# A hybrid attention backbone on one core: order of transposes, score products and output projection slices in layer 1's attention

## What is computed

```python
def attend_gqa(q, k, v):
    s = jnp.einsum('bqhgd,bkhd->bhgqk', q, k).astype(jnp.float32) * HEAD_SCALE
    p = jax.nn.softmax(s, axis=-1).astype(v.dtype)
    return jnp.einsum('bhgqk,bkhd->bqhgd', p, v)

# neighbourhood_attention, per row block:
        s_loc = jnp.einsum('bjqhd,bijkhd->bhjqik', q_row, k_sub).astype(jnp.float32) * HEAD_SCALE
        s_loc = jnp.where(col_mask[:, :, None, :], s_loc + bias[None].astype(jnp.float32), NEG_INF)
        s_ctx = jnp.einsum('bjqhd,bkhd->bhjqk', q_row, k_ctx).astype(jnp.float32) * HEAD_SCALE
        p = jax.nn.softmax(jnp.concatenate([s_ctx, s_loc], axis=-1), axis=-1).astype(v.dtype)

# odd_mixer (layer 1):
    def merge(o_gqa, o_na):
        return jnp.concatenate([o_gqa.reshape(b, t, -1), o_na.reshape(b, t, -1)], axis=-1) @ w_out
```

## Time and profile before

| | us |
|---|---|
| median of 3 runs | 1727.03 (1725.92 to 1727.90) |
| profiled execution, device time | 1728.22 |
| its span on the core | 1726.4 |
| outside the span | 1.8 |
| PE busy | 1656.3 (96% of the span) |
| DVE busy | 1093.7 (63%) |
| ACT busy | 675.6 (39%) |
| POOL busy | 156.8 (9%) |
| layer 1's attention, first scores to first projection matmul | 1169.51 to 1301.70 |

### The profile page before, as it was taken

How to read it: one execution, slowest core, us unless ns; L and a number is a source line. 1 busy time by engine, 2 the same in 40 slices (tenths; PEclk the granted TensorE clock), 3 DMA queues, 4 the chain that set the end, 5 groups by cost and what they waited for, 6 DMA issues and landing times.

```text
span 1726.4 us, 27094 instructions
## 1 busy us (share of the span) xinstructions
PE 1656.3 (96%) x10508; PEld 1464.7 (85%) x10508; DVE 1093.7 (63%) x1959; ACT 675.6 (39%) x1292; POOL 156.8 (9%) x171
## 2 busy tenths in 40 slices
PE   6999999999989999999999999998999899999997
PEld 4999788778979889899899878997779788888885
DVE  5889687673565675675675787715684754444446
ACT  4433467763463122122122165315673632222221
POOL 1000365230000000000000000003340000000000
PEclk9999999999999999999999999999999999999998
DMA  8434430013012332332333303103022122222221
GB/s 333 180 120 147 111 80 19 20 50 147 25 57 91 147 147 98 146 138 105 146 120 123 143 23 104 50 1 99 1 92 105 50 98 98 98 98 97 97 97 49
DMA packets 30259, 170.39 MB, mean 99 GB/s; under 512 B 3920, under 2 KB 6864, under 8 KB 12112
## 3 DMA queue, kind: packets, MB, share of 16 engines
q1 hardware_dynamic: 30160, 169.03, 27.3%
HBM read 156.17 MB, written 2.10 MB: 92 GB/s over the span
## 4 chain that ended last, share of the span: by engine, by line
PE 83%; DVE 9%; issue 3%; ACT 3%; DMA 1%; POOL 0%; SPq 0%; DVEq 0%; ACTq 0%
PE ps L1129 24%; PE ps L898 14%; PE ps L900 14%; PE ps L899 14%; PE ps L950 3%; PE ps L1065 2%; PE ps L964 2%; PE ps L1040 2%; PE ps L984 1%; PE ps L979 1%; PE ps L1028 1%; DVE nmax L2517 1%; PE ps L1018 1%; DVE h L2188 1%; PE ps L817 1%
## 5 line engine op out<-in xcount | busy, mean ns | idle before, releaser
L1489 ACT ACTIVATE whi<-raw 128x2048 fp32r<-128x2048 f32 x83 | 158.5, 1910 | 309.8 <-PE ps L900 281.9
L2034 DVE TENSOR_TENSOR wlo<-raw,whi 128x2048 fp32r<-128x2048 f32 x83 | 190.1, 2290 | 118.4 <-ACT whi L1489 118.1
L898 PE MATMUL ps<-whi,uhi 128*128 128x512 f32 x640 | 249.9, 390 | 0.4 <-DVE wlo L2034 0.4
L899 PE MATMUL ps<-wlo,uhi 128*128 128x512 f32 x640 | 249.1, 389 | 0.0
L900 PE MATMUL ps<-whi,ulo 128*128 128x512 f32 x640 | 249.1, 389 | 0.0
L1129 PE MATMUL ps<-ahi,whi 128*128 128x384 f32 (+1 forms) x720 | 215.3, 353 | 1.1 <-ACT relu L1877 1.1
L1129 PE MATMUL ps<-ahi,wlo 128*128 128x384 f32 (+1 forms) x720 | 215.2, 352 | 0.0
L1129 PE MATMUL ps<-alo,whi 128*128 128x384 f32 (+1 forms) x720 | 215.2, 352 | 0.0
L2452 DVE SCALAR_TENSOR_TENSOR ada_junk<-raw,silu_rows 128x1024 bf16<-128x1024 f32 x160 | 195.5, 1222 | 25.6 <-DMA raw<-in_w_ada_t 23.0
L898 PE MATMUL ps<-whi,ahi 128*128 128x256 f32 x592 | 170.1, 287 | 5.3 <-DVE alo L2149 2.4
L900 PE MATMUL ps<-whi,alo 128*128 128x256 f32 x592 | 167.5, 283 | 0.0
(11 more groups left out here) (252 smaller groups left out, 3071.4 us busy)
## 6 DMA issues: line engine op xcount, KB each, us to landing
raw<-in_w_ff SPq DMA_DIRECT2D x64, 1024.0 KB, 4.8
raw<-in_w_ada_t SPq DMA_DIRECT2D x40, 1024.0 KB, 4.8
raw<-in_w_in_odd SPq DMA_DIRECT2D x9, 1024.0 KB, 4.8
first_raw<-in_w_ada SPq DMA_DIRECT2D x8, 1024.0 KB, 21.5
raw<-in_w_in_even SPq DMA_DIRECT2D x8, 1024.0 KB, 4.9
h<-in_x SPq DMA_DIRECT2D x4, 1024.0 KB, 7.7
raw<-in_w_out_even SPq DMA_DIRECT2D x4, 1024.0 KB, 6.0
raw<-in_na_bias SPq DMA_DIRECT2D x4, 1024.0 KB, 5.0
```

The source lines that it names most:

```text
L898: pe.matmul(dst, lhs[0], rhs[0], start=first, stop=False)
L899: pe.matmul(dst, lhs[0], rhs[1], start=False, stop=False)
L1489: act.activation(whi[w % 2][:, :, :], raw[r % 2][:, :, :], ACT.Copy).then_inc(s_hi, 1)
L2034: dve.tensor_tensor(wlo[w % 2][:, :, :], raw[r % 2][:, :, :], whi[w % 2][:, :, :].bitcast(F32), ALU.subtract).then_inc(s_lo, 1)
```

## The change

Three edits, all in layer 1.

1. In steps i = 4, 6, ..., 30 and i = 32, 33, 34, PE does `probs_t(i-3)` ahead of `scores(i)` in place of behind it.
2. In the same steps DVE does `probs_a(i-3)` ahead of `maxima(i)` and `inverses(i-1)` in place of behind them. ACT's and POOL's order isn't touched.
3. Slices 0, 1 and 2 of the output projection's first unit are issued at the ends of steps 48, 49 and 50 of PE's loop, each behind the value product of that step. Ahead of each stand waits for all exponentials (`s_e1`) and for the 16 grouped-query outputs (`s_l1`), and in the product the wait for `wlo`. `output_projection` begins with slice 3.

No instruction that computes is added or removed.

```diff
             def odd_attention(tail):
...
                 for i in range(N_ODD + 5):
+                    turned_first = 4 <= i < N_GQA and i % 2 == 0 or N_GQA <= i < N_GQA + 3
+                    if turned_first:
+                        probs_t(i - 3)
                     if i < N_ODD:
                         scores(i)
-                    if 3 <= i < N_ODD + 3:
+                    if 3 <= i < N_ODD + 3 and not turned_first:
                         probs_t(i - 3)
                     if 4 <= i < N_ODD + 4 and (i - 4 >= N_GQA or i % 2 == 1):
                         values(odd_value_of(i - 4))
+                    if i in tail:
+                        tail[i]()
...
-                    product = first_products(w0, g, act, nt)
-                    pe.wait_ge(s_e1, N_ODD)
-                    pe.wait_ge(s_l1, N_GQA // 2)
-                    for k in range(KT):
+                    act = out1_act
+                    for k in range(3, KT):
                         if k == 4:
                             pe.wait_ge(s_l1, N_GROUPS)
-                        product(k, 0)
+                        out1_product(k, 0)
...
+            out1_product = first_products(W_OUT1, G_OUT1, out1_act, NTL)
+
+            def early_out1(k):
+
+                def run():
+                    pe.wait_ge(s_e1, N_ODD)
+                    pe.wait_ge(s_l1, N_GQA // 2)
+                    out1_product(k, 0)
+                return run
+
+            odd_attention({N_ODD + j: early_out1(j) for j in range(3)})
...
                 for i in range(N_ODD + 5):
+                    copied_first = 4 <= i < N_GQA and i % 2 == 0 or N_GQA <= i < N_GQA + 3
+                    if copied_first:
+                        probs_a(i - 3)
                     if i < N_ODD:
                         maxima(i)
                     if 1 <= i <= N_ODD:
                         inverses(i - 1)
-                    if 3 <= i < N_ODD + 3:
+                    if 3 <= i < N_ODD + 3 and not copied_first:
                         probs_a(i - 3)
```

More of the change, by code:

```diff
@@ L1005, in even_attention, with odd_attention @@
                         tail[i]()
-            def odd_attention():
+            def odd_attention(tail):
                 def scores(i):
@@ L1368, in output_projection @@
                 else:
-                    act = lambda part, k, a: ((gqa_hi, gqa_lo), (na_hi, na_lo))[k // 4][part][:, k % 4, a]
-                    product = first_products(w0, g, act, nt)
-                    pe.wait_ge(s_e1, N_ODD)
-                    pe.wait_ge(s_l1, N_GQA // 2)
-                    for k in range(KT):
+                    act = out1_act
+                    for k in range(3, KT):
                         if k == 4:
                             pe.wait_ge(s_l1, N_GROUPS)
-                        product(k, 0)
+                        out1_product(k, 0)
                 pe.wait_ge(s_lo, w0 + 2)
@@ L1396, in _ @@
             pe.wait_ge(s_gf, G_OUT1)
-            odd_attention()
+            out1_act = lambda part, k, a: ((gqa_hi, gqa_lo), (na_hi, na_lo))[k // 4][part][:, k % 4, a]
+            out1_product = first_products(W_OUT1, G_OUT1, out1_act, NTL)
[6 more added lines that the diff above has]
+            odd_attention({N_ODD + j: early_out1(j) for j in range(3)})
             output_projection(1, W_OUT1, G_OUT1)
```

## The result

The changed kernel takes 1718.77 us (median of 6 runs, 1718.24 to 1721.67), against 1726.55 us for the kernel before beside it (6 runs): 7.8 us less. The ratio is 0.9952 with a 95% interval of 0.9943 to 0.9962, that is 6.6 to 9.8 us. The forecast was 7.2 us less.

A forecast was written before the change was run, and what follows sets the result against it. TensorE, busy 96% of the span, was taken as the bound, stalling on DVE's copy; 6.5 us from edits 1 and 2 plus 0.7 from edit 3 gave 7.2, so 1727.03 - 7.2 = 1719.8 us, range 1718.2 to 1723.1.

The forecast's parts named there:

- The loop of before: Grouped-query rounds before the change: a turning waits for DVE's copy, taken behind the maxima; terms sum to 4.82 us per period.
- Entry: At step 4 the turning now ahead of the scores waits for an unmoved copy, so these scores start 1.3 us later.
- Period: One grouped-query period (two steps) after edits 1 and 2: 4.35 us in place of 4.82, set by the wait.
- The two claims: Two sums for the new grouped-query period: TensorE's own work 4.27 us, the wait for DVE's copy 4.34 us.
- The first claim: TensorE's own work in one new grouped-query period, two score products, two turnings and a value product, sums to 4.27 us.
- The rival that TensorE alone sets the period: Grouped-query loop: period 4.27 us, another 1.0 us saved, so 1718.8 us; chance 0.18.
- Steps 32 to 36: From the turning that opens step 32 to the scores of step 36: 11.61 us, with a new 1.0 us stall.
- Edits 1 and 2 together: Whole attention up to the scores of step 36: these scores come 6.5 us earlier than before.
- Edit 3: End of the attention: slice 0 fills a 0.97 us wait for POOL; saves 0.7 us, bounds 0 and 1.0.
- The slower rivals: Grouped-query loop: POOL paces it, 1735 us if DVE's scans shut POOL out, chance 0.03; or DVE's copy is late, 0.15.
- The late copy: Grouped-query loop: DVE's second copy comes later as ACT's exponential slips; period 4.6 us, 1723.1 us; chance 0.15.
- The low end of the range: Whole kernel: TensorE sets the period and the slices give 1.0 us, 1718.2 us.

## Why the prediction was right, point by point

*The loop of before.* Right. Its cause, the copy behind the maxima, is shown: with the copy moved alone the period falls to 4.56.

*Entry.* Forecast S(4) 1.30 later, since T(1) waits ahead of it; measured 1.30 (7.35 against 6.05 behind the first scores).

*Period.* Forecast 4.35, measured 4.33. The two claims were put at 4.27 (TensorE) and 4.34 (wait). The second stands as a sum, by terms that partly cancel: I had the exponential of e decide when DVE can take its reciprocal, 2.06 behind the maxima of e. That came at 2.01 (1198.56 - 1196.55), as the exponential starts 0.99 and not 1.04 behind the maxima, and at 2.01 DVE's own queue arrives there too. From the copy to the next turning I took 0.64, and it is 0.66 (1199.30 - 1198.64). As measured: 1.58 + 2.01 + 0.08 + 0.66 = 4.33. The first claim, TensorE alone, was 0.04 short, since I took a turning behind a value product for one behind scores; by the run with the copy ahead of the reciprocal it is 4.31. The number of changes of tiling mode in a period did stay at two, but I took from it that the sum stays, and the turning that now stands behind the value product pays 0.05 there. The rival that TensorE alone sets the period was given 1718.8, and the time did come out there; but the reason it gave is wrong, as its 4.27 doesn't exist (4.31 is what TensorE needs), and in the changed kernel the two claims are 0.02 apart.

*Steps 32 to 36.* Forecast 11.61 from T(29) to S(36), measured 11.58. The step that failed in between is T(31), put at 5.18 with no wait; it came at 5.92. I had followed DVE's queue and left out that ACT's copy of T(30) stands behind the exponentials of 32. The end was right nonetheless, since S(35), put at 8.07 and measured at 8.04, hangs on the exponentials of round 33 anyway, which the run with ACT's copy early shows.

*Edits 1 and 2 together.* Forecast 6.5, measured 6.79: 13 periods that were 0.02 shorter each give it.

*Edit 3.* Forecast 0.7, measured 0.38, inside its bounds of 0 to 1.0. Mechanism right, size off in two terms: from the end of the split to the first matmul I took 0.05, and it is 0.26 (1286.30 less 1283.76 and 2.28), for a cause that stays open (last section); and a slice between other work costs about 0.1 more than in the stream, which slices 1 and 2 pay for waits of 0.1 that they fill. 0.7 - 0.2 - 0.1 = 0.4.

*The slower rivals.* POOL has its 0.91 pieces at 1193.33 and 1194.49 in the changed kernel, each done before its turning: it doesn't pace. The one at 1193.33 lies beside DVE's maxima of 1193.34 and isn't stretched, so DVE's scans don't shut POOL out either. The late copy didn't come about: ACT's exponential starts 0.99 behind the start of DVE's maxima (1197.54 - 1196.55).

*Median.* 1718.77 lies 1.0 under the forecast of 1719.8. The traces give 7.13 us for the change, the forecast 7.2; the rest is within the interval of the ratio. The low end of the range, 1718.2, doesn't follow from its terms: TensorE alone (1718.8) and slices worth 1.0 in place of 0.7 make 1718.5. Nothing hangs on it here.

## What to carry to other kernels

Where two engines hand a single buffer back and forth, the order on both has to change together: the producer earlier and the consumer's copy ahead of its long scans. Here DVE's order alone gave 3.8 us, both 6.7, and PE's alone cost 13. When a loop's wait is removed, add up both the next wait and the busy engine's own list; if they are within a few hundredths, an edit that shortens only one of the two can give no more than that difference per period. A stall seen in a trace is worth what the next chain leaves of it: one of 0.69 us here was worth nothing.

## What the runs showed of the hardware

DVE's subtraction with two SBUF inputs and POOL's scaling exclude each other, in both directions: beside the 2.28 us split POOL's two pieces took 3.46 us (2.78 of it the second), apart from it 1.36; and when POOL was under way first, the split took 2.60. The Trainium skill, "SBUF — State Buffer", Who interferes with whom, states this lock; here the numbers agree with it, and no other DVE work of these rounds stretched POOL (0.91 in every period).

A turning of 6 transposes needs 0.63 us to the next scores when it stands behind a value product, and 0.58 behind scores; in the changed kernel, where it has also waited for the copy, it is 0.60 (1195.57 - 1194.97).

From the end of DVE's split to slice 0, which waited for it, passed 0.26 us, in each kernel with an early slice. That is not what such a wait costs in general: at three other places of the changed kernel's trace TensorE waits for a split, and its first matmul follows the end after 0.05 (1320.29 less 1317.95 and 2.29; 1042.51 less 1040.17 and 2.29; 987.78 less 985.44 and 2.29). After DVE's copy a turning that waited follows by 0.09 (1173.31 less 1172.68 and 0.54). What sets slice 0 apart in the rows is that it stands behind a value product, while the other three stand behind matmuls of their own kind; T(46) of before, also behind a value product, follows the end of POOL's pieces after 0.19 (1296.49 less 1292.84 and 3.46). No run here separates this from the further waits that stand ahead of slice 0, so the cause is open.
